# A two-layer decoder trunk: dense down projection in three split passes, and modulation sections spread over both layers

## Chip, cores and metric

The kernel runs on one core of a Trainium2 chip. The metric is the device time of one execution in microseconds (us).

## The reference

Two layers work on x, 256 tokens of 1024 channels in float32. A vector c, through silu, gives for each layer a modulation of six sections of 1024 values: `mod = silu(c) @ ada_w[l] + ada_b[l]`. Sections are numbered 6l + 0 to 6l + 5: shift, scale and gate of the mixer, then shift, scale and gate of the channel mixer.

```
for l in 0, 1:
    sh1, sc1, g1, sh2, sc2, g2 = split(mod[l], 6)
    h = rmsnorm(x) * (1 + sc1) + sh1
    x = x + g1 * hybrid_mixer(h)                 # nine 512-column projections, three gates of 1024, three branches, w_o
    h = rmsnorm(x) * (1 + sc2) + sh2
    layer 0: x = x + g2 * ((silu(h @ w1) * (h @ w3)) @ w2)       # D_FF = 2816: 22 tiles of 128
    layer 1: x = x + g2 * top-2-of-8 experts, each the same SwiGLU
out = rmsnorm(x)
```

## The kernel before, in words

Weights come from DRAM in pieces of 128x1024 float32 (512 KB). `dense_pieces` (L160) writes their order out by hand; the SP queue issues them in that order into a ring of RAW = 11 buffers (`raw`, L445 to L451), and waits before each until the piece 11 places ahead has been used up (`released`, L428). There are three kinds:

- "split" pieces. ScalarE (ACT) copies the piece to its rounded high part (L1049, called in `high_parts`), VectorE (DVE) takes the difference as the low part (L1237, in `low_parts`), both into a ring of SPL = 6 buffers (`split`); the raw buffer is free once the low part is there. TensorE (PE) then does three products for every tile: high by high, high by low, low by high (`PASSES`). A tile is one 128x128 weight block against 256 tokens, so a piece has 8 tiles and 24 matmuls.
- "ada" pieces, a 128-row part of a modulation section. DVE multiplies the piece by 128 values of silu(c) and adds to `adacc` (`product`, L1296). After eight of them PE sums over the partitions (`ada_sum`, L660) and DVE adds the bias (`modulate`, L1312). The first product of the next section waits for the sum of the last one.
- "down" pieces, the rows of w2 of layer 0, which PE reads from the raw buffer as plain float32, without a split (`next_direct`, L605; `down`, L826). The trace counts each such matmul as two instructions.

Each layer runs `norm`, then nine head groups (f, q, ab, ac, ah, i, v, u, g; four pieces each) with nine small score levels between them, then for each of three branches eight gate pieces and four branch pieces, then eight pieces of w_o. In layer 0 section 2 lies beside the head (four pieces after f, four after u), 3 and 4 beside the gates of branches c and b. Fifteen 512 KB blocks of zeros are written to DRAM in layer 1 on the same SP queue, one behind every second split piece from the first branch piece on (L452 to L455).

Layer 0 then has `dense_ffn` (L802): 11 pairs of tiles, four split pieces a pair (two of w1, two of w3), each pair followed by FFN_TAKE ada pieces: 4, 4, then 3 eight times, then 0, for the sections 5, 6, 7 and 11. A section is summed at the end of the pair after the one in which its products end. DVE first makes the low parts of the next pair, then the two products of each tile (L1605, L1607) when PE has finished the pair, then the ada products. The down projection follows: 22 pieces, with three sections (8, 9, 10) of ada pieces between them and three sums. The last four pieces are done bank by bank so that the residual add and the squares of the next norm can start early. Layer 1 has no sections of its own; its mixer and then the experts (528 pieces) follow.

PE works through two plans written out in order: units (four banks `psU`) and events (two pairs of banks `psA`); opening one waits until the one four units or two events earlier was emptied.

Of the kernel before, what the change touches and what calls it, by code (L numbers as in the profile page):

```python
# [109 lines left out]
def event_plan():  # L110

    plan = []
    for l in range(DEPTH):
# [5 lines left out]
        if l == 0:  # L119
            plan += [(("ada", s), "D") for s in (2, 3, 4)]  # L120
# [14 lines left out]
def unit_signals():  # L135
# [24 lines left out]
def dense_pieces():  # L160
# [18 lines left out]
    for l in range(DEPTH):  # L179
        for g in HEAD_GROUPS:  # L180
# [16 lines left out]
        if l == 0:  # L197
# [7 lines left out]
            for f in range(NF):  # L205
                out += [(("down", f), "ffn_w2", 0, f * P, 0, PIECE)] + ada[:DOWN_TAKE[f]]
# [13 lines left out]
DIRECT_POS = [pos for pos, p in enumerate(PIECES) if p[0][0] == "down"]  # L220
# [8 lines left out]
def program(nc, x, c, ada_w, ada_b, norm_mix_w, norm_ffn_w, w_in, conv_w, lb_logits, hgrn_norm_w,  # L229
# [3 lines left out]
    with ExitStack() as ctx:  # L233
# [25 lines left out]
        sig = sb("sig", [P, 4, 512])  # L259
        work = sb("work", [P, 10, 1024])  # L260
# [39 lines left out]
        hidden0 = work[:, 0:6, :].rearrange("p a b -> p (a b)")[:, 0:NF * T].rearrange("p (f t) -> p f t", t=T)  # L300
# [27 lines left out]
        s_down = sem("down_piece_used")  # L328
# [91 lines left out]
        def _(sp):  # L420
# [7 lines left out]
            def released(pos):  # L428
# [8 lines left out]
                elif use[0] == "mod":  # L437
                    sp.wait_ge(s_mpc, use[1] + 1)
                elif use[1] < NF - 1:
                    sp.wait_ge(s_down, use[1] + 1)  # L440
                else:
                    sp.wait_ge(s_ev, EVENT_AT["down1"] + 1)
# [63 lines left out]
        def _(pool):  # L506
# [38 lines left out]
            pool.memset(stored[:, :], 0.0).then_inc(s_ye, 1)  # L545

# [27 lines left out]
        def _(pe):  # L574
            units, events, pieces, direct = [0], [0], [0], [0]
# [28 lines left out]

            def next_direct():  # L605

                pos = DIRECT_POS[direct[0]]
                direct[0] += 1
                pe.wait_ge(s_raw[pos % RAW], 16 * (pos // RAW + 1))
                return raw[:, pos % RAW, :]  # L610
# [40 lines left out]
            def stat_pair(bank, count, j):  # L651
# [5 lines left out]
                if j == 3:  # L657
                    last.then_inc(s_ev, 1)

# [78 lines left out]
            def mixer(l):  # L738
# [25 lines left out]
                for n, b in enumerate(BRANCHES):  # L764
# [13 lines left out]
                    if l == 0 and n < 2:  # L778
                        ada_sum(2 + n)
# [4 lines left out]
                if l == 0:  # L784
                    ada_sum(4)
# [16 lines left out]
            def dense_ffn():  # L802
# [23 lines left out]
                def down(f, w, ms):  # L826
                    for m in ms:
                        last = mm(four[m // 2][:, (m % 2) * T:(m % 2 + 1) * T], w[:, m * P:(m + 1) * P],
                                  hidden0[:, f, :], f == 0 and m % 2 == 0, f == NF - 1)
                    return last  # L830

                for f in range(BANKWISE):
                    w = next_direct()
                    if f % 2 == 0:
                        pe.wait_ge(s_uD, emptied(UNITS, UNIT_AT[("ffn", f + 1)], "D"))
                    down(f, w, range(KD)).then_inc(s_down, 1)
                    if f in (6, 12, 17):
                        ada_sum(DOWN_ADA[f // 6 - 1 if f < 17 else 2])
                pe.wait_ge(s_uD, emptied(UNITS, UNIT_AT[("ffn", NF - 1)], "D"))
                ws = [next_direct() for _ in range(BANKWISE, NF)]  # L840
                for j in range(4):
                    if j == 3:
                        stat, _ = open_event((1, "norm1"))
                        for jj in range(2):
                            stat_pair(stat, 3, jj)
                    for f, w in zip(range(BANKWISE, NF), ws):
                        last = down(f, w, (2 * j, 2 * j + 1))
                        if j == 3 and f < NF - 1:
                            last.then_inc(s_down, 1)
                    last.then_inc(s_dn if j % 2 == 0 else s_ev, 1)  # L850
# [93 lines left out]
            assert (units[0], events[0], pieces[0], direct[0]) == (len(UNITS), len(EVENTS), NSPLIT, len(DIRECT_POS))  # L944
# [65 lines left out]
        def _(act):  # L1010
# [20 lines left out]
            def unit(key):  # L1031
# [4 lines left out]
                elif key[0] == "ffn":  # L1036
                    upto = min(used + 4, SIGNAL["ffn", NF - 1][2])
# [26 lines left out]
            def norm(l, second):  # L1064

                used = SIGNAL[l, "wo", 3][2] if second else SIGNAL["ffn", NF - 1][2] if l else 0
                std(early[:, 2 * l + second:2 * l + second + 1], eps[:, :], 1)
                if l and not second:
                    high_parts(used + SPL)
# [12 lines left out]
                high_parts(used + (SPL if l or second else 4))  # L1082
# [137 lines left out]
        def _(dve):  # L1220
# [20 lines left out]
            def unit(key):  # L1241
                kind, count, used = SIGNAL[key]
                upto = used + AHEAD - 1
                if key[0] in ("ffn", "mod"):
                    upto = min(upto, SIGNAL["ffn", NF - 1][2])
# [121 lines left out]
            def prepare(l, j):  # L1367
# [8 lines left out]
                settle()  # L1376
                if j == 1:
# [45 lines left out]
            def mixer(l):  # L1423
# [454 lines left out]
```

## Time and profile before

| | us |
|---|---|
| median of 3 runs | 1616.83 (1615.46 to 1622.0) |
| the profiled execution's own time | 1616.18 |
| its span in the trace | 1614.6 |
| PE busy in the span | 1553.5 (96%) |
| DVE busy | 1268.7 (79%) |
| ACT busy | 928.8 (58%) |

The profile's page gives for each engine the busy time and its share of the span, a view of 40 equal slices with one digit each, the chain of waits that ended last, and groups of instructions by line. Where a helper issues all instructions (L596 for matmuls, L1049 for ACT's copies), the tile's name tells the groups apart. Layer 0's mixer lies at about 42 to 309 us, the pairs of the dense channel mixer at 314 to 463, the down projection at 463 to 553, layer 1's mixer at 558 to 817, and the experts behind it.

### The profile page before, as it was taken

The numbers are of one execution on the slowest core, as the hardware profiler recorded it, in microseconds if no ns is written. First come the engines' busy times: TensorE is split into PE (matmuls) and PEld (weight loads), VectorE is DVE, ScalarE is ACT, GpSimd is POOL, SyncE is SP. The second block draws the span as 40 slices with busy tenths as digits, with TensorE's granted clock in tenths as the row PEclk, the third lists the DMA queues.
The fourth block names the chain that finished last, engine by engine and source line by source line (L and its number), as shares of the span: only waits on it lengthen the run. The fifth ranks groups of instructions, "written<-read, shape, count | busy, mean of one in ns | idle before, by whom it ended". The sixth has DMA issues, their size and how long they took to land.

```text
span 1614.6 us, 26010 instructions
## 1 busy us (share of the span) xinstructions
PE 1553.5 (96%) x9478; PEld 1335.6 (83%) x9478; DVE 1268.7 (79%) x1464; ACT 928.8 (58%) x1060; POOL 37.6 (2%) x45
## 2 busy tenths in 40 slices
PE   6999999899899899999979999999999999999997
PEld 5998999899898799999977777777777777777775
DVE  7786878667664559666649989989898998989897
ACT  3534544523310343544448878787777878777784
POOL 0000000000000000000003000000000000000200
PEclk7999999999999999999979999999999999999999
DMA  8943879368789734686619999999999999999993
GB/s 330 311 131 105 274 261 294 111 209 274 259 302 320 265 116 134 202 280 227 204 53 333 395 384 391 388 379 367 388 367 383 377 375 379 364 388 371 384 390 155
DMA packets 258574, 468.97 MB, mean 290 GB/s; under 512 B 15732, under 2 KB 129580, under 8 KB 258500
## 3 DMA queue, kind: packets, MB, share of 16 engines
q1 hardware_dynamic: 252608, 455.66, 79.9%
q0 software_dynamic: 3248, 11.11, 1.9%
q10 hardware_dynamic: 2644, 1.18, 0.3%
q8 instruction: 50, 0.82, 0.2%
q14 instruction: 24, 0.20, 0.0%
HBM read 453.90 MB, written 14.00 MB: 290 GB/s over the span
## 4 chain that ended last, share of the span: by engine, by line
PE 71%; DVE 6%; DMA 2%; issue 1%; ACT 1%; DVEq 0%; SPq 0%
PE psU L596 48%; PE psA L596 22%; DMA raw<-in_ffn_w_dram 2%; DVE adacc L1310 2%; PE psA L966 1%; DVE split L1237 1%; PE psU L904 0%; DVE merged L1339 0%; DVE sig L1605 0%; PE psU L926 0%; ACT split L1049 0%; DVE rstd L1333 0%; DVE split L1648 0%; DVE sc L1404 0%; DVE work L1477 0%
## 5 line engine op out<-in xcount | busy, mean ns | idle before, releaser
L1049 ACT ACTIVATE split<-raw 128x1024 fp32r<-128x1024 f32 x732 | 765.1, 1059 | 431.0 <-PE psU L596 192.6
L1648 DVE TENSOR_TENSOR split<-raw,split 128x1024 fp32r<-128x1024 f32 x528 | 615.4, 1220 | 21.1 <-ACT split L1049 19.2
L596 PE MATMUL psU<-hS,split 128*128 128x256 f32 x3936 | 493.3, 288 | 23.2 <-DVE hS L1357 13.7
L596 PEld LDWEIGHTS psU<-hS,split 128*128 128x128 f32 x3936 | 485.9, 196 | 26.6 <-issue 26.0
L596 PE MATMUL psU<-split,xE 128*104 128x512 f32 (+1 forms) x2304 | 496.6, 375 | 2.3 <-DVE xE L1775 2.3
L596 PEld LDWEIGHTS psU<-split,xE 128*104 128x104 f32 x2304 | 365.9, 168 | 119.6 <-issue 2.4
L1237 DVE TENSOR_TENSOR split<-raw,split 128x1024 fp32r<-128x1024 f32 x204 | 242.0, 1219 | 66.5 <-ACT split L1049 66.2
L596 PE MATMUL psA<-split,hidE 128*104 128x512 f32 x1056 | 249.2, 395 | 0.0
L596 PEld LDWEIGHTS psA<-split,hidE 128*104 128x104 f32 x1056 | 175.4, 168 | 63.9
L1310 DVE SCALAR_TENSOR_TENSOR adacc<-raw,cact,adacc 128x1024 f32<-128x1024 f32 x70 | 89.8, 1283 | 10.1 <-DMA raw<-in_ada_w_dram 4.9
L596 PE MATMUL psA<-work,raw 128*128 128x256 f32 x352 | 78.8, 386 | 0.5 <-DVE mod L1318 0.5
L596 PEld LDWEIGHTS psA<-work,raw 128*128 128x128 f32 x352 | 67.7, 193 | 10.0 <-DVE mod L1318 0.5
L596 PE MATMUL psU<-yS,split 128*128 128x256 f32 x576 | 70.1, 283 | 0.0
L596 PEld LDWEIGHTS psU<-yS,split 128*128 128x128 f32 x576 | 69.6, 192 | 0.0
L1806 DVE TENSOR_TENSOR hidE<-psA,hidE 128x416 fp32r<-128x416 f32 (+1 forms) x48 | 26.6, 554 | 37.7 <-ACT hidE L1049 37.7
L596 PE MATMUL psU<-split,hS 128*128 128x512 f32 x192 | 45.8, 394 | 2.2 <-DVE split L1237 2.2
L596 PEld LDWEIGHTS psU<-split,hS 128*128 128x128 f32 x192 | 35.5, 188 | 10.2 <-issue 3.0
L1136 ACT ACTIVATE sig<-psU 128x512 f32<-128x512 f32 x24 | 14.3, 595 | 50.6 <-PE psU L596 46.0
L1049 ACT ACTIVATE hidE<-psA 128x416 fp32r<-128x416 f32 (+1 forms) x48 | 23.4, 488 | 31.0 <-PE psA L966 31.0
L1186 ACT ACTIVATE sig<-psU 104x512 f32<-104x512 f32 (+1 forms) x48 | 27.0, 562 | 14.8 <-PE psU L596 14.8
L1799 DVE TENSOR_TENSOR sig<-sig,psU 104x512 f32<-104x512 f32 (+1 forms) x48 | 30.5, 635 | 3.6 <-PE psU L596 3.6
L596 PE MATMUL psA<-work 128*128 128x128 f32 x272 | 33.2, 275 | 0.0
(217 smaller groups left out, 728.3 us busy)
## 6 DMA issues: line engine op xcount, KB each, us to landing
raw<-in_moe_w_dram SPq DMA_DIRECT2D x528, 512.0 KB, 7.2
raw<-in_w_in_dram SPq DMA_DIRECT2D x120, 512.0 KB, 5.9
raw<-in_ada_w_dram SPq DMA_DIRECT2D x96, 512.0 KB, 7.4
raw<-in_ffn_w_dram SPq DMA_DIRECT2D x66, 512.0 KB, 6.0
raw<-in_w_o_dram SPq DMA_DIRECT2D x16, 512.0 KB, 6.3
token_rows<-sc SPq DMA_DIRECT2D x10, 512.0 KB, 6.9
raw<-in_w_br_a_dram SPq DMA_DIRECT2D x8, 512.0 KB, 6.8
raw<-in_w_br_c_dram SPq DMA_DIRECT2D x8, 512.0 KB, 8.5
```

The costliest lines, as they stand in the source:

```text
L596: return pe.matmul(o, a, b, start=start, stop=stop, skip_group_check=True)
L966: last = pe.transpose(T_BANKS[g % 2][:, m * CAP:(m + 1) * CAP], sig[0:CAP, 2 + g % 2, m * P:(m + 1) * P], ident[0:CAP, 0:CAP])
L1049: return act.activation(o, i, ACT.Copy)
L1136: act.activation(sig[:, j, :], bank[:, :], ACT.Sigmoid).then_inc(s_uA, 1)
L1186: act.activation(sig[0:CAP, g % 2, 0:width], psU[2 * (g % 2)][0:CAP, 0:width], ACT.Silu).then_inc(s_silu, 1)
L1237: TTN(split[:, n % SPL, 1, :], raw[:, SPLIT_POS[n] % RAW, :], split[:, n % SPL, 0, :].bitcast(F32), ALU.subtract).then_inc(s_lo, 1)
L1310: STT(adacc[:, :], raw[:, pos % RAW, :], cact[:, k:k + 1], adacc[:, :], ALU.mult, ALU.add).then_inc(s_afree, 1)
L1648: TTN(split[:, slot, 1, :], raw[:, (RAW0 + n) % RAW, :], split[:, slot, 0, :].bitcast(F32), ALU.subtract).then_inc(s_lo, 1)
L1799: TTN(sig[0:CAP, 2 + g % 2, 0:width], s, three, ALU.mult).then_inc(s_hrow, 1)
L1806: TTN(h_lo, T_BANKS[g % 2][:, 0:len(tiles) * CAP], h_hi.bitcast(F32), ALU.subtract).then_inc(s_hlo, 1)
```

## The change

Pieces of w2 become split pieces. The hidden tiles get a high part (`hid_hi`, ACT copies it) and a low part (`hid_lo`, DVE subtracts), and the down projection does three passes. ACT computes Silu itself in place of Sigmoid, so DVE has one multiply for a tile and one subtraction. The hidden tiles lie in memory that `work` and `yS` use at other times; POOL clears part of `work` before layer 1 (`s_cleared`). The last three pieces, not four, go bank by bank. Sections 8, 9 and 10 move to layer 1, at the places where 2, 3 and 4 lie in layer 0; section 11 moves beside the down projection, one ada piece behind every second piece; 5, 6 and 7 stay beside the pairs, 3, 3 and 2 pieces a pair, so that each ends with a pair. The load of the final norm's weights moves from the down projection to behind section 10.

```diff
-FFN_ADA = [5, 6, 7, 11]
-DOWN_ADA = [8, 9, 10]
-BANKWISE = NF - 4
-DOWN_TAKE = [2, 2, 1, 1, 1, 1] * 3 + [0] * (NF - 18)
+FFN_ADA = [5, 6, 7]
+DOWN_ADA = [11]
+LAST_ROWS = 3
+BANKWISE = NF - LAST_ROWS
+MOD_AT = 18
+DOWN_TAKE = [int(f % 2 == 0 and f < 2 * KD) for f in range(NF)]
-FFN_TAKE = [4, 4] + [3] * 8 + [0]
+FFN_TAKE = [3, 3, 2] * 3 + [0, 0]
...
-        if l == 0:
-            plan += [(("ada", s), "D") for s in (2, 3, 4)]
+        plan += [(("ada", 6 * l + s), "D") for s in (2, 3, 4)]
...
+            used += MOD_AT if kind == "mod" else 0
             signal[key] = ("direct", direct, used)
+            used += NF - MOD_AT if kind == "mod" else 0
...
-            if l == 0 and g == "f":
+            if g == "f":
                 two = section()
                 out += two[:4]
-            if l == 0 and g == "u":
+            if g == "u":
                 out += two[4:]
...
-            ada = section() if l == 0 and b != BRANCHES[0] else []
+            ada = section() if b != BRANCHES[0] else []
...
-                out += [(("down", f), "ffn_w2", 0, f * P, 0, PIECE)] + ada[:DOWN_TAKE[f]]
+                out += [("split", "ffn_w2", 0, f * P, 0, PIECE)] + ada[:DOWN_TAKE[f]]
...
+        with ExitStack() as ffn:
+            hid_hi = ffn.enter_context(nc.sbuf_tensor("hid_hi", [P, NF + 2, T], F32R))
+            hid_16 = ffn.enter_context(nc.sbuf_tensor("hid_16", [P, 16, T], F32R))
         work = sb("work", [P, 10, 1024])
...
-        hidden0 = work[:, 0:6, :].rearrange("p a b -> p (a b)")[:, 0:NF * T].rearrange("p (f t) -> p f t", t=T)
+        hid_lo = [hid_16[:, f, :] for f in range(16)] \
+            + [yS[:, f // HB, f % HB, :] for f in range(NF - 16)]
...
-            pool.wait_ge(s_unit, SIGNAL["mod", 10][1])
-            pool.dma_start(fwbc, final_norm_w.rearrange("(a d) -> a d", a=1).to_broadcast([P, D])).then_inc(s_fw, 16)
-
+            pool.wait_ge(s_ev, EVENT_AT["down1"] + 1)
+            pool.memset(work[:, 4:6, :], 0.0).then_inc(s_cleared, 1)
...
+            pool.wait_ge(s_ev, EVENT_AT[("ada", 10)] + 1)
+            pool.dma_start(fwbc, final_norm_w.rearrange("(a d) -> a d", a=1).to_broadcast([P, D])).then_inc(s_fw, 16)
...
-                    if l == 0 and n < 2:
-                        ada_sum(2 + n)
+                    if n < 2:
+                        ada_sum(6 * l + 2 + n)
...
-                if l == 0:
-                    ada_sum(4)
+                ada_sum(6 * l + 4)
...
-                        last = mm(four[m // 2][:, (m % 2) * T:(m % 2 + 1) * T], w[:, m * P:(m + 1) * P],
-                                  hidden0[:, f, :], f == 0 and m % 2 == 0, f == NF - 1)
+                        for wp, hp in PASSES:
+                            last = mm(four[m // 2][:, (m % 2) * T:(m % 2 + 1) * T], w[wp][:, m * P:(m + 1) * P],
+                                      hid_lo[f] if hp else hid_hi[:, f, :], f == 0 and m % 2 == 0 and (wp, hp) == (0, 0),
+                                      f == NF - 1 and (wp, hp) == PASSES[-1])
                     return last
 
                 for f in range(BANKWISE):
-                    w = next_direct()
-                    if f % 2 == 0:
-                        pe.wait_ge(s_uD, emptied(UNITS, UNIT_AT[("ffn", f + 1)], "D"))
-                    down(f, w, range(KD)).then_inc(s_down, 1)
-                    if f in (6, 12, 17):
-                        ada_sum(DOWN_ADA[f // 6 - 1 if f < 17 else 2])
-                pe.wait_ge(s_uD, emptied(UNITS, UNIT_AT[("ffn", NF - 1)], "D"))
-                ws = [next_direct() for _ in range(BANKWISE, NF)]
+                    pe.wait_ge(s_flo, f + 1)
+                    w = next_split()
+                    down(f, w, range(KD)).then_inc(s_used, 1)
+                    if f == MOD_AT - 1:
+                        ada_sum(DOWN_ADA[0])
+                pe.wait_ge(s_flo, NF)
+                ws = [next_split() for _ in range(BANKWISE, NF)]
...
+            def ffn_high(f):
+
+                act.wait_ge(s_uD, emptied(UNITS, UNIT_AT[("ffn", f)], "D"))
+                copy(hid_hi[:, f, :], sig[:, f % 4, T:2 * T]).then_inc(s_fhi, 1)
+
             for f in range(NF):
                 bank = unit(("ffn", f))
-                act.activation(sig[:, f % 4, 0:T], bank[:, 0:T], ACT.Sigmoid).then_inc(s_sig, 1)
+                act.activation(sig[:, f % 4, 0:T], bank[:, 0:T], ACT.Silu).then_inc(s_sig, 1)
+                if f:
+                    ffn_high(f - 1)
+            ffn_high(NF - 1)
+            high_parts(FFN_END + NF)
...
-                if l == 0:
-                    for k in range(4):
-                        product(2, k)
+                for k in range(4):
+                    product(6 * l + 2, k)
...
+            def ffn_low(f):
+
+                dve.wait_ge(s_fhi, f + 1)
+                TTN(hid_lo[f], sig[:, f % 4, T:2 * T], hid_hi[:, f, :].bitcast(F32), ALU.subtract).then_inc(s_flo, 1)
+
...
-                link(TTN(sig[:, f % 4, 0:T], sig[:, f % 4, 0:T], bank[:, 0:T], ALU.mult))
-                settle()
-                TTN(hidden0[:, f, :], sig[:, f % 4, 0:T], bank[:, T:2 * T], ALU.mult).then_inc(s_uD, 1)
+                TTN(sig[:, f % 4, T:2 * T], sig[:, f % 4, 0:T], bank[:, T:2 * T], ALU.mult).then_inc(s_uD, 1)
+                if f:
+                    ffn_low(f - 1)
...
+            ffn_low(NF - 1)
             modulate(FFN_ADA[-1])
-            for s in DOWN_ADA:
-                for k in range(KD):
-                    product(s, k)
-                modulate(s)
-
-            dve.wait_ge(s_eD, emptied(EVENTS, EVENT_AT[("ada", 11)], "D"))
-            low_parts(SIGNAL["ffn", NF - 1][2] + SPL)
+            done = 0
+            for f in range(NF):
+                low_parts(FFN_END + f + 1)
+                for _ in range(DOWN_TAKE[f]):
+                    product(DOWN_ADA[0], done)
+                    done += 1
+            modulate(DOWN_ADA[0])
+
+            dve.wait_ge(s_eD, emptied(EVENTS, EVENT_AT[("ada", 5)], "D"))
+            low_parts(FFN_END + NF + SPL - LAST_ROWS)
```

## Rows read from the trace of the kernel before

**Rows 1.** Windows by stage: mixer of layer 0, pairs, down projection.

```profile
core 0: us, PE busy (x) PEld busy (x) DVE busy (x) ACT busy (x) POOL busy (x), PEclk, DMA share, GB/s
42.10:308.70 266.60, 263.46 (x2076) 257.00 (x2076) 205.56 (x250) 119.26 (x141) 1.38 (x1) 0.99 0.69 223
313.60:463.20 149.60, 140.52 (x1104) 139.33 (x1104) 104.45 (x125) 48.92 (x63) 0.00 (x0) 0.94 0.69 232
463.20:553.40 90.20, 88.95 (x433) 78.12 (x432) 41.44 (x47) 11.10 (x14) 0.76 (x1) 0.98 0.85 300
```

**Rows 2.** Waits of PE, 313 to 466 us: total, times, longest.

```profile
PE psU L596 <- DVE split L1237: 8.2, 5, 3.8
```

**Rows 3.** Waits of DVE in the same stretch.

```profile
DVE mod L1318 <- PE psA L596: 6.2, 2, 3.8
```

**Rows 4.** Timeline of PE, pairs: start, length, instruction, count [idle before <- releaser].

```profile
313.70 36.60 PE L596 MATMUL psU<-hS,split 128*128 128x256 f32 x288 [5.01 <-DVE hS L1357]
...
437.61 25.70 PE L596 MATMUL psU<-hS,split 128*128 128x256 f32 x192 [3.76 <-DVE split L1237]
463.25 1.95 PE L596 MATMUL psA<-ones,adacc 128*128 128x1 f32 x16
```

**Rows 5.** Chain of waits, 400 to 421 us: start, length, step.

```profile
401.98 1.29 DVE adacc L1310
...
406.06 5.21 DMA raw<-in_ffn_w_dram
411.29 1.07 ACT split L1049
...
415.10 1.29 DVE adacc L1310
```

**Rows 6.** Timeline at the end of the last pair, all engines.

```profile
463.35 0.66 ACT L1151 ACTIVATE sig<-psU 128x256 f32<-128x256 f32 x2 [6.42 <-PE psU L596]
463.83 0.42 DVE L1605 TENSOR_TENSOR sig<-sig,psU 128x256 f32<-128x256 f32 x1 [0.64 <-ACT sig L1151]
```

**Rows 7.** Timeline of PE, down projection.

```profile
465.67 26.10 PE L596 MATMUL psA<-work,raw 128*128 128x256 f32 x112 [0.48 <-DVE mod L1318]
491.61 1.84 PE L596 MATMUL psU<-ones,adacc 128*128 128x1 f32 x16
493.31 20.97 PE L596 MATMUL psA<-work,raw 128*128 128x256 f32 x96
514.11 1.84 PE L596 MATMUL psU<-ones,adacc 128*128 128x1 f32 x16
```

**Rows 8.** Timeline of PE, layer 1, gates and branch c.

```profile
720.32 23.20 PE L596 MATMUL psU<-hS,split 128*128 128x256 f32 x192
743.36 11.68 PE L596 MATMUL psU<-yS,split 128*128 128x256 f32 x96
```

**Rows 9.** The page, costliest groups: busy, mean ns of one.

```profile
L1049 ACT ACTIVATE split<-raw 128x1024 fp32r<-128x1024 f32 x732 | 765.1, 1059 | 431.0 <-PE psU L596 192.6
L1237 DVE TENSOR_TENSOR split<-raw,split 128x1024 fp32r<-128x1024 f32 x204 | 242.0, 1219 | 66.5 <-ACT split L1049 66.2
```

**Rows 10.** Timeline of PE: first and last matmuls of mixer 0, then of mixer 1.

```profile
42.19 25.47 PE L596 MATMUL psU<-hS,split 128*128 128x256 f32 x192 [3.62 <-DVE hS L1357]
67.50 1.03 PE L859 MATMUL psU<-ident,work 128*128 128x128 f32 x8
...
307.56 1.13 PE L596 MATMUL psA<-sig,ones 128*128 128x256 f32 x4 [0.77 <-ACT sig L1078]
...
558.52 30.96 PE L596 MATMUL psU<-hS,split 128*128 128x256 f32 x240 [5.11 <-DVE hS L1357]
...
816.27 1.13 PE L596 MATMUL psA<-sig,ones 128*128 128x256 f32 x4 [0.77 <-ACT sig L1078]
```

**Rows 11.** Windows: gates b of layer 0; zero blocks of layer 1 (PE, PEclk, DMA share, GB/s).

```profile
248.00:281.00 33.00, 33.00 (x279) 33.00 (x277) 27.48 (x29) 15.11 (x18) 0.00 (x0) 1.00 1.05 341
...
733.00:738.00 5.00, 5.00 (x44) 1.00 0.95 291
```

More of the change, by code:

```diff
@@ L219 @@
 ZERO_AT = {SPLIT_POS[NSPLIT - 4 * (3 * len(BRANCHES) + 2) + 8 + 2 * n]: b for n, b in enumerate(ZERO_BLOCKS)}
-DIRECT_POS = [pos for pos, p in enumerate(PIECES) if p[0][0] == "down"]
+FFN_END = SIGNAL["ffn", NF - 1][2]
 assert len(SPLIT_POS) == NSPLIT and len(ADA_POS) == NADA * KD - len(DIRECT1 + DIRECT0)
@@ L326, in program @@
         s_out = sem("out_stored")
-        s_down = sem("down_piece_used")
+        s_fhi = sem("ffn_tile_high")
+        s_flo = sem("ffn_tile_low")
+        s_cleared = sem("level_operands_cleared")
         s_dn = sem("down_first_bank_of_pair_ready")
@@ L436, in released @@
                     sp.wait_ge(s_ev, EVENT_AT[("ada", 0)] + 1)
-                elif use[0] == "mod":
+                else:
                     sp.wait_ge(s_mpc, use[1] + 1)
[L439 to L442, printed above, removed]
             sp.wait_ge(s_small, 16 * len(stacks))
@@ L574, in _ @@
         def _(pe):
-            units, events, pieces, direct = [0], [0], [0], [0]
+            units, events, pieces = [0], [0], [0]
             def open_unit(key):
@@ L603, in next_split @@
                 return split[:, n % SPL, 0, :], split[:, n % SPL, 1, :]
[L605 to L610, printed above, removed]
             PASSES = ((0, 0), (0, 1), (1, 0))
@@ L658, in stat_pair @@
                     last.then_inc(s_ev, 1)
+                return last
             def ada_sum(s):
@@ L843, in dense_ffn @@
                         stat, _ = open_event((1, "norm1"))
-                        for jj in range(2):
-                            stat_pair(stat, 3, jj)
+                        stat_pair(stat, 3, 0)
                     for f, w in zip(range(BANKWISE, NF), ws):
[L847 to L850, printed above, removed]
+                        if j == 3:
+                            down(f, w, (6,))
+                            last = down(f, w, (7,))
+                            last.then_inc(s_used if f < NF - 1 else s_ev, 1)
+                        else:
+                            last = down(f, w, (2 * j, 2 * j + 1))
+                    if j < 3:
+                        last.then_inc(s_dn if j % 2 == 0 else s_ev, 1)
+                stat_pair(stat, 3, 1).then_inc(s_used, 1)
                 for jj in range(2, 4):
@@ L943, in _ @@
             gather(open_event("gather0")).then_inc(s_ev, 1)
-            assert (units[0], events[0], pieces[0], direct[0]) == (len(UNITS), len(EVENTS), NSPLIT, len(DIRECT_POS))
+            assert (units[0], events[0], pieces[0]) == (len(UNITS), len(EVENTS), NSPLIT)
             pe.wait_ge(s_uA, emptied(UNITS, len(UNITS), "A"))
@@ L1036, in unit @@
                 elif key[0] == "ffn":
-                    upto = min(used + 4, SIGNAL["ffn", NF - 1][2])
+                    upto = used + 4
                 if used:
@@ L1064, in norm @@
             def norm(l, second):
-                used = SIGNAL[l, "wo", 3][2] if second else SIGNAL["ffn", NF - 1][2] if l else 0
+                used = SIGNAL[l, "wo", 3][2] if second else FFN_END + NF if l else 0
                 std(early[:, 2 * l + second:2 * l + second + 1], eps[:, :], 1)
                 if l and not second:
-                    high_parts(used + SPL)
+                    high_parts(used + SPL - LAST_ROWS)
                 for j in range(4):
@@ L1081, in norm @@
                 std(rstd[:, :], bank[:, 0:T], D).then_inc(s_eA, 1)
-                high_parts(used + (SPL if l or second else 4))
+                high_parts(used + (SPL if second else 4))
                 if not (l or second):
@@ L1243, in unit @@
                 upto = used + AHEAD - 1
-                if key[0] in ("ffn", "mod"):
-                    upto = min(upto, SIGNAL["ffn", NF - 1][2])
                 if used:
@@ L1376, in prepare @@
                 settle()
+                if l and j == 1:
+                    dve.wait_ge(s_cleared, 1)
                 if j == 1:
@@ L1514, in ada_part @@
                 def ada_part(n, ks):
-                    gates = SIGNAL[(0, "gate" + BRANCHES[n], 0)][2] - 2
-                    if l == 0:
-                        for k in ks:
-                            if n:
-                                low_parts(gates + k + 1)
-                            product(2 + n, k)
+                    gates = SIGNAL[(l, "gate" + BRANCHES[n], 0)][2] - 2
+                    for k in ks:
+                        if n:
+                            low_parts(gates + k + 1)
+                        product(6 * l + 2 + n, k)
                 ada_part(0, range(4, KD))
@@ L1576, in mixer @@
                                 merged_low(3)
-                    if l == 0 and n < 2:
-                        modulate(2 + n)
-                if l:
-                    unit_done(("mod", 8))
-                else:
-                    modulate(4)
-                    dve.wait_ge(s_eD, emptied(EVENTS, EVENT_AT[("ada", 2)], "D"))
+                    if n < 2:
+                        modulate(6 * l + 2 + n)
+                modulate(6 * l + 4)
+                dve.wait_ge(s_eD, emptied(EVENTS, EVENT_AT[("ada", 6 * l + 2)], "D"))
                 for j in range(4):
```

## The prediction

> **What bounds the kernel now.** I read the page first: PE is busy for 96% of the span, so only PE's own work, its waits and its clock can move the end. I then cut the span into stages with the windows view [rows 1]; the reader is to see that the mixer of layer 0 has PE busy for nearly all of its 266.6 us at a clock of 0.99, while the pairs of the dense channel mixer have 9.1 us without PE work and a clock of 0.94. PE's waits in that stretch name the low parts of the weights, 8.2 us in five waits [rows 2]. DVE's own waits say why: twice it stood before `modulate` until PE had summed a section, 6.2 us [rows 3]. That is a section that ended in the middle of a pair: its sum runs only after the next pair, and until then DVE makes no low parts and frees no ada buffer. The chain of waits shows the second limit, a loop of 13.1 us a pair (401.98 to 415.10: three products, 5.21 us from the last release to the landing of a piece, the high part, the low part, the tiles) against the 11.5 us that PE needs [rows 5]. In the down projection PE hardly waits at all; there the work itself is the time.
>
> **Pace of PE.** At full clock 192 split matmuls of 128x256 take 743.36 - 720.32 = 23.04 us, 0.120 us each [rows 8]. The plain float32 ones of the down projection take 514.11 - 493.31 = 20.80 us for 96, 0.217 each, and there are two in the trace for each matmul written [rows 7]. A section's sum costs 493.31 - 491.61 = 1.70 us [rows 7].
>
> **The pairs (313.7 to 463.25, 149.5 us).** Work that stays: 1056 matmuls x 0.120 = 126.7; three sums (5, 6, 7), 5.1; the start, where 288 matmuls took 36.60 in place of 34.56, 2.0 [rows 4]. Together 133.8, so 15.7 us are waits and the slow clock behind them. The price of one such clock dip: behind the 3.76 us wait the last 192 matmuls took 463.25 - 437.61 = 25.64 us, 2.6 more than at full clock [rows 4, 8]. With 3, 3 and 2 ada pieces each section ends with a pair and the next one starts a pair later, when its sum follows directly: the 6.2 us on DVE go. In the loop, the buffer for the fourth split piece two pairs on is freed by the third product in a pair (3, 3), by the second in (3, 2), and by the second of two in (2, 3); so two of three pairs have a loop shorter by 1.29 + 0.1, 11.7 us, and three pairs take 13.1 + 2 x 11.7 = 36.5 us against 3 x 11.5 + 1.7 = 36.2 of PE. That is even, and the first pairs have some slack, so I keep 4.5 us of residue (3.0 of waits, 1.5 of clock; bounds 0 and 12). The new ACT copies and DVE subtractions lie beside this: DVE still has two operations of 0.42 us a tile, and ACT is busy for 48.9 of 149.6 us and gets 22 copies of about half of 1.06 us or less [rows 1, 6, 9]; were the cover gone, their 22 x 0.5 = 11 us would show. After: 138.3. Gain 11.2.
>
> **The turn to the down projection.** PE opens its banks after `modulate(7)`, which now stands behind the last low part. Before, 465.67 - 463.25 = 2.42 us passed, with the sum of 11 inside [rows 4, 7]. Now the chain from 463.35 is: two Silus and the high copy between them, about 1.2 us; the last high copy and the latency around it, 0.6; the last subtraction 0.42; `modulate` 0.2; handing over, 0.6. That makes 3.2 us (bounds 2.4, and 4.5 if each copy takes as long as 0.66 us). PE comes out of it at a lower clock as behind a 3.76 us wait: 2.6 us.
>
> **The down projection (463.2 to 553.4, 90.2 us).** Removed: 352 x 0.217 = 76.4 at the steady pace (with the slow first group 465.67 to 491.61 it was 78.0), 5.1 for three sums, the 2.4 above. What is left, 4.7, is norm statistics and the last residual add, which stay. Added: 22 pieces x 24 matmuls x 0.120 = 63.4, one sum 1.7. After: 3.2 + 2.6 + 63.4 + 1.7 + 4.7 = 75.6, gain 14.6 (bounds 12 and 16). ACT's 22 x 1.06 = 23 us and DVE's 22 x 1.22 + 8 x 1.3 = 37 us [rows 5, 9] lie beside 63 us of PE; the transfers fall from 46 to 30 pieces in that stage, and a raw buffer is now freed when it is split, not when PE has used it. If the split were not hidden, a piece would cost 1.06 + 1.22 = 2.3 us, still under PE's 2.88. Three pieces held for the bank-wise end leave three of six split buffers for layer 1 where before all six were ready; layer 0 starts in that very way.
>
> **Layer 1.** Added: 24 products on DVE, 24 ada pieces in the queue, three sums on PE, a move of the ring's release by ada pieces. Layer 0 runs the same code with its sections already, so it is the nearest row: from its first matmul to the last statistic 308.69 - 42.19 = 266.50 us, in layer 1 817.40 - 558.52 = 258.88 [rows 10]. The difference is 7.6; of it 1.0 is the turning of the gating weights, which stays in layer 0. So +6.6, of which 5.1 are sums and the rest the start with fewer pieces ready. Layer 1 has besides fifteen blocks of zeros in the same queue, which layer 0 has not. I add 1.4 for them (bounds 0 and 29, below). POOL's clearing and the moved load of the final norm have tens of us before their users wait; SP and POOL are not passed by anything on PE's path. Sum: +8.0.
>
> **Sum.** 1616.18 - 11.2 - 14.6 + 8.0 = 1598.4 against the profiled execution's own time, which stands 0.65 under the median of the runs; I say 1599.
>
> **Zero blocks and a rule.** Beside the gates of branches c and b layer 1 will ask for 8 gate pieces, 8 ada pieces and 4 zero blocks each, 20 x 0.524 = 10.5 MB in 23.0 us. In layer 0, without zero blocks, the transfer engines are already full over such a stretch, share 1.05 at 341 GB/s [rows 11]; at that rate each takes 30.8 us, 7.7 too many. The lookahead covers it: eleven raw buffers, half of them split pieces, and up to five pieces split ahead, some ten pieces or 29 us, and behind each gate group four branch pieces with two zero blocks need only 9.2 of 11.5 us. The Trainium skill, page "DMA: Bandwidth & Descriptors", section "Specifications", speaks against the change here: it gives a core a limit of about 358 GB/s from HBM. By that rule a group would take an estimated 29.3 us, 6.3 too many, which by itself, without lookahead, makes 12.6 for both in place of the 15.4 that the row gives; the row's 341 is a little below the rule and I go by the row.
>
> **Rivals.** (A) The loop in the pairs stays as it is: 13.1 us a pair, because landings grow with the new order. For it: the landing is 5.2 us in one loop and set by what else is in flight. Against: fewer pieces, and no sums in mid-pair. Then the pairs gain about 3 in place of 11.2: 1607. (B) The zero blocks eat half of the lookahead: half of 15.4 in place of 1.4 and one clock dip, +9: 1608. For it: share 1.05 in layer 0; against: the ten pieces ahead. (C) Slower: with reads and writes mixed, the rate at the gates of layer 1 drops to the 291 GB/s of a five-us window among the zero blocks, with a share of 0.95 [rows 11]. A group then takes 36.0 us, 13 too many, 26 for both, and with the lookahead used up two dips of 2.6: +31 in place of 1.4, 1628. It decides from a stall of 19 us on (no faster) or 27 (slower by 0.5%). Against it: that window follows a pause in the releases, so its rate is not a limit. (D) The change does not do what it says: weights are loaded 528 times in place of 352, and if a load of about 0.19 us were not hidden, the down projection would take 528 x 0.19 = 100 us, 37 more: 1636. The same loads stand in the gates, at 0.120 a matmul [rows 8], so hardly.
>
> **Chances.** Forecast 0.72 (own range 1591 to 1606), A 0.12, B 0.09, C 0.05, D 0.02. A measurement of this kernel can tell about 0.5%, 8.1 us, from no change, so faster means under 1608.7. The forecast is faster throughout, A and B about two times in three: 0.72 + 0.14 = 0.86; same 0.09, slower 0.05. The range 1590 to 1609 takes in A and B.
>
> **What would show it.** Pairs: about 138 us with a clock near 0.98, and no wait of DVE on a sum; over 145 means A. Between the last pair's matmul and the first of the down projection 3 us. Down projection: 528 matmuls at 0.12, stage about 76. Layer 1 from its first matmul to the last statistic 267; over 275, with PE waiting for low parts beside `ada` or w_in landings at the gates, means B or C. Experts and layer 0 unchanged. I am wrong in the main step if the three passes run slower than 0.125 each, or if PE waits again for DVE between pieces of w2.

## The result and the profile after

The changed kernel takes 1591.04 us (median of 4 runs, 1590.47 to 1591.6) against 1616.14 us for the kernel before beside it: ratio 0.9844, 95% interval 0.9831 to 0.9857. The forecast was 1599; the way and the mechanism were right, the gain is 25 us where 17 were forecast.

The page of the changed kernel, its first part: busy time, share of the span, instructions.

```profile
span 1588.4 us, 26461 instructions
PE 1533.6 (97%) x9654; PEld 1325.9 (83%) x9654; DVE 1291.2 (81%) x1486; ACT 959.7 (60%) x1104; POOL 39.5 (2%) x46
```

PE's timeline over the pairs, to be laid beside [rows 4] (start, length, count, idle before):

```profile
314.16 48.01 PE L602 MATMUL psU<-hS,split 128*128 128x256 f32 x384 [5.01 <-DVE hS L1369]
362.00 1.84 PE L602 MATMUL psA<-ones,adacc 128*128 128x1 f32 x16
363.71 34.79 PE L602 MATMUL psU<-hS,split 128*128 128x256 f32 x288
...
436.37 11.75 PE L602 MATMUL psU<-hS,split 128*128 128x256 f32 x96
450.82 0.55 PE L602 MATMUL psA<-hid_hi,split 128*128 128x256 f32 x1 [2.69 <-DVE mod L1330]
...
454.80 0.40 PE L602 MATMUL psA<-hid_hi,split 128*128 128x256 f32 x2
```

From the first matmul of the pairs to their last there is no idle time left; the only wait behind that is the 2.69 us before the down projection. PE's waits there, the same stage in windows, and the chain of waits from 330 to 448 us, which is PE's own work alone, say it again (compare [rows 2] and [rows 1]):

```profile
PE psU L602 <- DVE hS L1369: 5.0, 1, 5.0
PE psA L602 <- DVE mod L1330: 2.7, 1, 2.7
```

```profile
314.00:448.10 134.10, 133.94 (x1104) 133.63 (x1104) 97.02 (x119) 60.13 (x86) 0.00 (x0) 0.99 0.75 255
```

```profile
by line: PE psU L602 95.8%; PE psA L602 4.3%
```

The end of the down projection, and the first and last matmuls of layer 1's mixer (compare [rows 7] and [rows 10]):

```profile
514.67 1.02 PE L602 MATMUL psA<-sig,ones 128*128 128x256 f32 x4
...
517.67 2.92 PE L602 MATMUL psA<-sig,ones 128*128 128x256 f32 x12
525.70 10.60 PE L602 MATMUL psU<-hS,split 128*128 128x256 f32 x72 [5.11 <-DVE hS L1369]
...
790.27 1.13 PE L602 MATMUL psA<-sig,ones 128*128 128x256 f32 x4 [0.76 <-ACT sig L1082]
```

Read from these rows and those of before, the span's 26.2 us (1614.6 to 1588.4) come apart like this:

| stage | before | forecast | after | moved |
|---|---|---|---|---|
| up to the first matmul of the pairs | 313.70 | 313.70 | 314.16 | +0.5 |
| pairs | 149.55 | 138.3 | 133.96 | -15.6 |
| turn and down projection to the last statistic | 90.2 | 75.6 | 72.5 | -17.7 |
| from there to layer 1's first matmul | 5.1 | 5.1 | 5.1 | 0 |
| layer 1, first matmul to last statistic | 258.88 | 266.9 | 265.70 | +6.8 |
| rest (routing, experts, end) | 797.2 | 797.2 | 797.0 | -0.2 |

### The profile page after: what moved, and what is told of

Read it like the earlier page. It is cut to its first block, busy times and chain, and to the rows that moved or that the text cites. A ratio compares the mean times of both kernels' runs of the same rounds, so it can differ in the third digit from the quotient of the medians.

```text
span 1588.4 us, 26461 instructions
## 1 busy us (share of the span) xinstructions
PE 1533.6 (97%) x9654; PEld 1325.9 (83%) x9654; DVE 1291.2 (81%) x1486; ACT 959.7 (60%) x1104; POOL 39.5 (2%) x46
## 4 chain that ended last, share of the span: by engine, by line
PE 74%; DVE 5%; issue 1%; ACT 0%; DVEq 0%
PE psU L602 51%; PE psA L602 22%; PE psA L970 1%; DVE split L1251 1%; DVE adacc L1322 0%; DVE merged L1351 0%; PE psU L908 0%; PE psU L930 0%; DVE rstd L1345 0%; DVE split L1666 0%; DVE sc L1418 0%; DVE work L1490 0%; DVE hS L1369 0%; DVE work L1870 0%; DVE work L1402 0%
## 5 line engine op out<-in xcount | busy, mean ns | idle before, releaser
L1053 ACT ACTIVATE split<-raw 128x1024 fp32r<-128x1024 f32 x754 | 788.2, 1059 | 378.3 <-PE psU L602 178.3
L1666 DVE TENSOR_TENSOR split<-raw,split 128x1024 fp32r<-128x1024 f32 x528 | 615.4, 1220 | 21.4 <-ACT split L1053 19.4
L602 PE MATMUL psU<-hS,split 128*128 128x256 f32 x3936 | 488.0, 286 | 16.3 <-DVE hS L1369 13.7
L602 PEld LDWEIGHTS psU<-hS,split 128*128 128x128 f32 x3936 | 480.6, 194 | 19.2 <-issue 18.2
L1251 DVE TENSOR_TENSOR split<-raw,split 128x1024 fp32r<-128x1024 f32 x226 | 268.7, 1219 | 66.1 <-ACT split L1053 65.6
L602 PE MATMUL psA<-hid_hi,split 128*128 128x256 f32 x352 | 64.9, 286 | 2.7 <-DVE mod L1330 2.7
L602 PEld LDWEIGHTS psA<-hid_hi,split 128*128 128x128 f32 x352 | 55.5, 193 | 2.9 <-DVE mod L1330 2.9
L602 PE MATMUL psA<-hid,split 128*128 128x256 f32 x128 | 36.6, 286 | 0.0
```

The lines of the kernel that those rows point to most:

```text
L602: return pe.matmul(o, a, b, start=start, stop=stop, skip_group_check=True)
L1053: return act.activation(o, i, ACT.Copy)
L1251: TTN(split[:, n % SPL, 1, :], raw[:, SPLIT_POS[n] % RAW, :], split[:, n % SPL, 0, :].bitcast(F32), ALU.subtract).then_inc(s_lo, 1)
L1666: TTN(split[:, slot, 1, :], raw[:, (RAW0 + n) % RAW, :], split[:, slot, 0, :].bitcast(F32), ALU.subtract).then_inc(s_lo, 1)
```

## The experiments

For a short comparison of all kernels, their traces are cut at three marks: D is the time from the first matmul of the pairs to ACT's square root behind the down projection (`rstd`), L from there to the same mark at the end of layer 1's mixer. The ratio is to the kernel before beside each. D and L come from one profile of each kernel. They hold some chance: the first 384 matmuls of the pairs, the same instructions with no wait among them, took 48.01 us in the change, 48.79 in e4 and e7, and 49.19 in e5, so a difference of up to 1.2 us in D need not be an edit's doing.

| kernel | median | ratio (95% interval) | D | L |
|---|---|---|---|---|
| before | | 1 | 239.8 | 264.0 |
| the change | 1591.04 | 0.9844 (0.9831 to 0.9857) | 206.5 | 270.8 |
| e1 three passes alone | 1621.34 | 1.0027 (1.0016 to 1.0038) | 246.1 | 264.0 |
| e1b the same, DVE's order capped | 1622.91 | 1.0042 (1.0028 to 1.0055) | 246.4 | 263.6 |
| e1c the same, ada pieces spread | 1612.61 | 0.998 (0.9969 to 0.999) | 235.3 | 264.2 |
| e2 sections alone | 1604.82 | 0.9927 (0.9908 to 0.9946) | 220.5 | 270.8 |
| e3 3 pieces a pair, ends in mid-pair | 1600.9 | 0.9898 (0.9875 to 0.9922) | 217.7 | 270.8 |
| e6 4 pieces a pair, ends on borders | 1607.74 | 0.995 (0.9932 to 0.9968) | 222.7 | 270.8 |
| e4 modulate(7) early | 1588.05 | 0.9825 (0.9807 to 0.9844) | 204.2 | 270.9 |
| e7 modulate(7) behind pair 9 | 1587.22 | 0.9817 (0.9802 to 0.9831) | 202.3 | 271.6 |
| e5 zero blocks twice | 1599.7 | 0.9895 (0.9878 to 0.9912) | 207.7 | 279.0 |
| e8 second statistic early | 1592.2 | one run | 208.0 | 270.8 |

### e1: the three passes alone

The changed kernel with the sections put back:

```
-FFN_ADA = [5, 6, 7]
-DOWN_ADA = [11]
-MOD_AT = 18
-DOWN_TAKE = [int(f % 2 == 0 and f < 2 * KD) for f in range(NF)]
-FFN_TAKE = [3, 3, 2] * 3 + [0, 0]
+FFN_ADA = [5, 6, 7, 11]
+DOWN_ADA = [8, 9, 10]
+MOD_AT = {8: 7, 9: 13, 10: 18}
+DOWN_TAKE = [2, 2, 1, 1, 1, 1] * 3 + [0] * (NF - 18)
+FFN_TAKE = [4, 4] + [3] * 8 + [0]
...
-                for k in range(4):
-                    product(6 * l + 2, k)
+                if l == 0:
+                    for k in range(4):
+                        product(2, k)
```

> The down projection in three passes, with the modulation sections placed as before (5, 6, 7, 11 beside the pairs; 8, 9, 10 beside the down projection; none in layer 1). Theory 1 (the two parts of the change add up, and each saves PE time by itself): the pairs stay at 149.5 us, the down projection falls from 90.2 to about 78 (63.4 of matmuls, 5.1 for three sums, turn, statistics), so 12 us less than before, 1604. Theory 2 (the sections have to go before three passes can pay): DVE has 22 low parts and 24 products there, 58 us, and their order and landings hold PE up; PE waits for low parts of w2 for 5 us or more and the kernel stays at 1609 or above.

Measured: 1621.34, slower than the kernel before. Theory 1 fell. The time is in the range of theory 2, which put it down to DVE's order and the landings; the next two kernels take these apart. PE's waits from 313 to 560 us:

```profile
PE psA L605 <- DVE mod L1335: 10.9, 1, 10.9
PE psU L605 <- DVE split L1256: 9.1, 6, 3.8
PE psA L605 <- DVE split L1256: 7.5, 2, 6.3
```

The waits in the pairs (second row) are those of before; the 10.9 us before the down projection and the 7.5 us in it are new. DVE's timeline there (start, length, count):

```profile
502.47 0.16 DVE L1335 TENSOR_TENSOR mod<-psU,vecs 128x8 f32<-128x8 f32 x1
502.54 0.75 DVE L1324 TENSOR_SCALAR adacc<-raw,cact 128x1024 f32<-128x1024 f32 x1
503.39 8.23 DVE L1327 SCALAR_TENSOR_TENSOR adacc<-raw,cact,adacc 128x1024 f32<-128x1024 f32 x6
511.54 1.22 DVE L1256 TENSOR_TENSOR split<-raw,split 128x1024 fp32r<-128x1024 f32 x1
```

Reading a section's bank (`unit`) first makes low parts up to four pieces ahead, and then the products of those pieces come in a row: nine microseconds without a low part, longer than PE's ready pieces last.

### e1b: the same with DVE's order capped

```
             def unit(key):
                 kind, count, used = SIGNAL[key]
                 upto = used + AHEAD - 1
+                if key[0] in ("ffn", "mod"):
+                    upto = min(upto, FFN_END)
```

> As e1, but DVE makes no low part of w2 ahead of the tiles of the last pair and none ahead of its products when it turns to a section's sum (the cap that the kernel before had in unit() stays). Theory 1 (e1 lost its gain to DVE's order: 10.9 us before the down projection and 7.5 us beside it while six products ran in a row): the wait before the down projection falls to 4 us or less, the waits between pieces of w2 below 3 us, the kernel comes to about 1606 to 1610. Theory 2 (24 products and 46 transfers beside the down projection cannot keep up with 2.88 us a piece in any order): the waits move but stay above 12 us together and the kernel stays above 1614.

Measured: 1622.91, no better: the numbers are those of theory 2 (waits above 12 us, time above 1614). The products no longer come six in a row, but the wait before the down projection is still 9.3 us (row: total, times, longest), and so theory 1's account of it, DVE's order, was wrong:

```profile
PE psA L605 <- DVE split L1256: 16.4, 3, 9.3
```

SP's queue and ACT in e1b around the end of the last pair, which PE leaves at 464.3 us:

```profile
462.30 0.33 SPq L458 DMA_DIRECT2D raw<-in_ffn_w_dram  x1
462.68 0.43 SPq L458 DMA_DIRECT2D raw<-in_ada_w_dram  x1
463.15 0.43 SPq L458 DMA_DIRECT2D raw<-in_ffn_w_dram  x1
...
467.78 1.06 ACT L1058 ACTIVATE split<-raw 128x1024 fp32r<-128x1024 f32 x1 [6.35 <-DMA raw<-in_ffn_w_dram]
470.63 1.06 ACT L1058 ACTIVATE split<-raw 128x1024 fp32r<-128x1024 f32 x1 [1.79 <-DMA raw<-in_ffn_w_dram]
471.59 0.36 ACT L1166 ACTIVATE sig<-psU 128x256 f32<-128x256 f32 x1
```

The third and fourth pieces of w2 are issued at 462.30 and 463.15, when the last pair is nearly over. With the sections of before, five ada pieces stand between the first four pieces of w2. So in a ring of eleven the third one needs the buffer of the last ada piece before the last pair, whose product ends at 462.27, and the fourth stands behind it in the queue. ACT makes high parts four pieces ahead before it turns to a tile, so the Silu of the last pair (471.59), and with it the whole turn, waits until the fourth piece has landed at about 470.6. The plain float32 reading of before split no piece of w2, so nothing stood in front of the tiles.

### e1c: the same with the ada pieces spread

```
-MOD_AT = {8: 7, 9: 13, 10: 18}
-DOWN_TAKE = [2, 2, 1, 1, 1, 1] * 3 + [0] * (NF - 18)
+MOD_AT = {8: 9, 9: 15, 10: 19}
+DOWN_TAKE = [0, 0] + [2, 1, 1, 1, 1, 1, 1] + [2, 1, 1, 2, 1, 1] + [2, 2, 2, 1, 1] + [0, 0]
```

> As e1b, but the 24 ada pieces beside the down projection are spread over pieces 2 to 19 of w2, none behind the first two, and each sum comes when DVE is just through with its section. Theory 1 (e1 and e1b lost to ada pieces between the first four pieces of w2, which set the wait before the down projection, and to bunched products): that wait falls from 9 us to about 3, the waits between pieces to 5 us or less, the kernel to 1608 to 1612. Theory 2 (46 transfers, 24.1 MB, and 58 us of DVE do not fit into 63 us of matmuls in this ring, however spread): PE waits stay above 12 us together, 1615 or more.

Measured: 1612.61, 0.998 of before. Theory 1 is nearly met, and theory 2 fell: from 463 to 545 us PE waits for low parts of w2 for 8.2 us in all, 5.4 us of it at the turn, where theory 1 said 3:

```profile
PE psA L605 <- DVE split L1256: 8.2, 6, 5.4
```

The order was worth 10 us, but no order that was tried brings the 12 us that the matmuls alone save.

### e2: the sections alone

On the kernel before, with the plan of the change for the sections (constants as in the diff, `ada_sum(6 * l + ...)`, `product(6 * l + ...)`, `modulate(6 * l + ...)`), w2 in plain float32 and four pieces bank by bank. Only the start of layer 1 has another number, since ada pieces now stand behind its first four split pieces:

```
-            low_parts(SIGNAL["ffn", NF - 1][2] + SPL)
+            low_parts(SIGNAL["ffn", NF - 1][2] + 3)
```

> The sections placed as in the change, the down projection left in plain float32 with four pieces bank by bank. Theory 1 (waits and slow clock in the pairs come from the placement of the sections): the pairs fall from 149.5 to about 134, the down projection loses two sums (3.4 us), layer 1 gains 6.8; together 12 us less than before, 1604. Theory 2 (the shorter vector chain of a tile, with Silu on ACT, is what freed the pairs): the pairs stay above 142, the kernel at 1610 or above.

Measured: 1604.82, as theory 1 has it. PE's timeline of the pairs is that of the change, with the two multiplies of a tile of before:

```profile
313.92 47.98 PE L594 MATMUL psU<-hS,split 128*128 128x256 f32 x384 [5.01 <-DVE hS L1354]
361.74 1.84 PE L594 MATMUL psA<-ones,adacc 128*128 128x1 f32 x16
363.44 34.79 PE L594 MATMUL psU<-hS,split 128*128 128x256 f32 x288
```

So the placement freed the pairs, not Silu. With e1 this shows that the two parts do not add up: sections alone -19.3 us in D, three passes alone +6.3 (-4.5 in e1c's order), both together -33.3. On top of the new placement the three passes bring 14.0.

### e3 and e6: where a section ends, and how many pieces a pair takes

```
-FFN_TAKE = [3, 3, 2] * 3 + [0, 0]
+FFN_TAKE = [3] * 8 + [0, 0, 0]          # e3
+FFN_TAKE = [4, 4] * 3 + [0] * 5         # e6
```

> The changed kernel with 3 ada pieces behind each of the first eight pairs in place of 3, 3, 2 behind nine: as many pieces in all, but sections 5 and 6 end in the middle of a pair. Theory 1 (DVE stands before a sum that comes only after the next pair): DVE waits on PE before modulate in two places, PE waits for low parts behind them for some 4 to 6 us with a slow clock after it, pairs at 140 to 145, the kernel 6 to 10 us above the change. Theory 2 (only the number of ada pieces per pair matters, by the loop): one piece less in the loop is all that 3, 3, 2 had; no wait on a sum, 0 to 2 us above the change.

> The changed kernel with 4 ada pieces behind each of the first six pairs and none behind the other five: sections end on pair borders, but the loop from product to tile is one product longer. Theory 1 (only the sums in mid-pair made PE wait; the loop of 14.4 us is drawn against slack and ends after six pairs): no wait of DVE on a sum, 0 to 3 us above the change. Theory 2 (the loop sets the pace, as the prediction's residue of 4.5 us had it): 14.4 against 11.5 us a pair over six pairs, PE waits for low parts 6 us or more, the kernel 8 us or more above the change.

e3 measured 1600.9, 10 us above the change: theory 1. DVE's and PE's waits in e3's pairs:

```profile
DVE mod L1330 <- PE psA L602: 11.0, 2, 6.0
```

```profile
PE psU L602 <- DVE split L1251: 6.4, 3, 3.5
```

Two sections end in mid-pair, and there are two waits of DVE on a sum; D grows by 11.2 us, of which 6.4 are PE's waits. The other 4.8 are for the most part the low clock behind them: the 192 matmuls behind the waits of 2.15 and 3.54 us took 24.75 and 25.84 us, where [rows 8] has 23.20.

e6 measured 1607.74, 17 us above the change. Theory 1 fell and theory 2 holds: no wait of DVE on a sum, but the loop costs more than the mid-pair ends. PE's waits and a piece of the chain in e6 (start, length, step):

```profile
PE psU L602 <- DVE split L1251: 10.5, 4, 3.1
```

```profile
333.38 1.30 DVE adacc L1322
334.69 0.37 SPq L455
335.11 7.34 DMA raw<-in_ffn_w_dram
342.48 1.06 ACT split L1053
...
350.20 1.30 DVE adacc L1322
```

The loop takes 350.20 - 333.38 = 16.8 us, not the 14.4 of both theories: four products free four buffers one after the other, and the piece that counts lands after 7.3 us, where it was 5.2 in [rows 5]. In the kernel before, too, the pieces behind the four products of its first two pairs land after 7.27 and 6.54 us. That the piece then stands behind others in the queue is the likely reason; no run isolates it. Both limits that the prediction named are real; the change clears both at once.

### e4 and e7: the turn to the down projection

```
                 TTN(sig[:, f % 4, T:2 * T], sig[:, f % 4, 0:T], bank[:, T:2 * T], ALU.mult).then_inc(s_uD, 1)
+                if f == NF - 2:                 # e4
+                    modulate(FFN_ADA[-1])
                 if f:
                     ffn_low(f - 1)
+                if f == NF - 3:                 # e7, in place of the one above
+                    modulate(FFN_ADA[-1])
...
             ffn_low(NF - 1)
-            modulate(FFN_ADA[-1])
```

> The changed kernel with DVE's modulate(7) moved from behind the last low part of the hidden tiles to the first tile of the last pair, where its sum has long been there. Theory 1 (PE's 2.7 us before the down projection are the chain up to modulate, which only frees a bank, and the slow clock behind it costs about 1 us more): PE starts the down projection within 0.7 us of the last pair, the kernel is 3 to 4 us below the change. Theory 2 (the first pieces of w2 or the low part of the hidden tiles set the start): 0 to 1 us.

> The changed kernel with modulate(7) right behind the tiles of the last but one pair, so that nothing of the last pair stands before PE's start on the down projection. Theory 1 (only the bank's release held PE; the first hidden tiles and pieces of w2 are long ready): PE goes on within 0.2 us, 4 us below the change and 1 us below e4. Theory 2 (the first pieces of w2 or DVE's wait for the sum take its place): as e4 or slower.

Both as theory 1 has them, e4 with 1.1 us of waiting left instead of 0.7. PE's wait in e4:

```profile
PE psA L602 <- DVE mod L1330: 1.1, 1, 1.1
```

The clock behind the wait, first in the change, then in e4 (us, PE busy, clock, transfer share, GB/s):

```profile
448.20:453.20 5.00, 2.38 (x11) 0.76 0.14 13
```

```profile
448.20:453.20 5.00, 4.47 (x38) 1.00 0.17 35
```

In e7 PE goes from the last pair, whose last matmul ends at 448.2, into the down projection with no wait at all:

```profile
448.07 0.28 PE L602 MATMUL psA<-hid_hi,split 128*128 128x256 f32 x1
```

D is 4.2 us under the change's, although e7's first 384 matmuls took 0.8 us more. From the end of the pairs to the square root it is 5.0 us (448.12 to 520.63 in the change, 448.22 to 515.77 in e7). Of these 2.7 are the wait. The clock is 1.6: the change's first 20 matmuls behind the wait take from 450.82 to 454.80, 3.98 us in place of 2.4. The rest is a slightly quicker pace at full clock that e4 does not have, so it is not the edit's. At 0.9817 it is the fastest kernel of the study; its interval overlaps e4's.

### e5: the room in layer 1's queue

```
                     sp.dma_start({"x": xrows, "y": yrows}[table][row:row + P, :], scf[:, 0:D]).then_inc(s_fill, 16)
+                    again = ZERO_BLOCKS.index((table, row)) * P
+                    sp.dma_start(morerows[again:again + P, :], scf[:, 0:D]).then_inc(s_fill, 16)
```

> The changed kernel with each block of zeros in layer 1 written twice, the second time to rows of its own that nobody reads: 15 more transfers of 512 KB in the stretch of the gates. Theory 1 (the transfers of layer 1 are covered by the lookahead, with room left): 0 to 3 us above the change, PE waits for weights in layer 1 stay below 6 us. Theory 2 (the rate near 341 GB/s is already used up beside the gates, rival B of the prediction nearly happened): 15 x 0.524 MB / 341 GB/s = 23 us more transfer time, of which 10 us or more show.

Measured: 1599.7, 9 us above the change, between the two: 8.2 in L. PE's waits in layer 1, and the windows of the stretch (us, busy times, clock, transfer share, GB/s):

```profile
PE psU L605 <- DVE split L1254: 8.2, 3, 5.9
```

```profile
660.00:755.00 95.00, 88.24 (x719) 87.92 (x720) 69.27 (x72) 36.95 (x42) 0.00 (x0) 0.96 1.01 380
```

One wait of 5.9 us is new, late in the stretch; the other 2.3 us are two waits that the change has too. Behind the new wait the next 96 matmuls take 13.51 us in place of 11.75, so the low clock makes most of the rest of the 8.2. Of 7.9 MB more, 21 us at 380 GB/s, more than half still did not show. Not only the lookahead took it up: in the change SP issues nothing from 681.1 to 692.0 us, since it waits for a buffer, and the transfers stand nearly still (share 0.17, 40 GB/s):

```profile
685.00:695.00 10.00, 10.00 (x87) 10.00 (x87) 6.59 (x9) 2.12 (x2) 0.00 (x0) 1.00 0.17 40
```

As an estimate, 21 less 8 us at 1.4 us a transfer, the change has room for some nine more transfers.

### e8: the order of the statistics

```
                         stat_pair(stat, 3, 0)
+                        stat_pair(stat, 3, 1)
...
-                stat_pair(stat, 3, 1).then_inc(s_used, 1)
-                for jj in range(2, 4):
-                    stat_pair(stat, 3, jj)
+                stat_pair(stat, 3, 2).then_inc(s_used, 1)
+                stat_pair(stat, 3, 3)
```

> The changed kernel with the second statistic of the norm again ahead of the last bank's matmuls, as in the kernel before. Theory 1 (three statistics behind the last matmul fill the time in which DVE and ACT make the last squares, which was 0.77 us of waiting): a wait of PE of 0.8 us on ACT's squares comes back and the stage from the last pair to the last statistic takes 0.8 to 1 us more than in the change. Theory 2 (the shorter stage comes from elsewhere): no such wait, no difference.

In e8's PE waits the one of before is back, and PE's timeline shows what it costs:

```profile
PE psA L602 <- ACT sig L1082: 0.8, 1, 0.8
```

```profile
515.10 1.89 PE L602 MATMUL psA<-sig,ones 128*128 128x256 f32 x8
...
518.95 1.02 PE L602 MATMUL psA<-sig,ones 128*128 128x256 f32 x4
520.75 1.13 PE L602 MATMUL psA<-sig,ones 128*128 128x256 f32 x4 [0.77 <-ACT sig L1082]
```

From the first statistic to the end of the last it is 515.10 to 521.88, 6.8 us, against 514.67 to 520.59, 5.9 us, in the change, with the same matmuls between: 0.9 us, as theory 1 has it. The whole stage from the last pair on takes only 0.4 us more, since the matmuls before it ran a little quicker. D is 208.0 against 206.5, but 1.1 of these 1.5 us lie in the first 384 matmuls of the pairs (49.13 against 48.01) and have nothing to do with the edit.

## Why the prediction was right, and where it was off

- **The bound.** Right: PE's waits and clock in the pairs and its work in the down projection are where the time went. Layer 0 and the experts moved by 0.5 and 0.2 us.
- **The pairs.** Mechanism right, size off. Of the 15.7 us named as waits and slow clock all 15.6 went; the residue of 4.5 us was not there. The step that mis-sized it is the loop, "13.1 + 2 x 11.7 = 36.5 us against 3 x 11.5 + 1.7 = 36.2". It treated a loop that is as long as PE's work as one that must stall; the chain of the change from 330 to 448 us is PE's own work alone. That the first pairs give slack and the last two have no ada pieces is the likely reason, which no run shows by itself. e6 shows that the loop is no phantom: one product more in it costs 17 us, and its landing is longer behind four products than behind three. e3 shows the other half, sums in mid-pair. That DVE's new tile chain would cost nothing was right (e2 has the old one and the same pairs).
- **The turn.** 2.70 us for 3.2. It was rightly seen as `modulate(7)` behind the low parts. The clock behind it cost 1.6 us, less than the 2.6 taken from the last pairs of before. e7, which has neither, is 5.0 us shorter in the stage.
- **The down projection.** 63.4 us of matmuls was close: from 450.82 to 520.59 it is 69.8 us, and without 1.6 of slow clock, 1.7 for the sum and 3.6 for the statistics 62.9 are left, 0.119 for each of 528. The stage holds no waits. The statistics were called unchanged at 4.7 us and take 517.67 to 520.59 and 0.67 before, 3.6: three stand behind the last matmul now and fill a wait of 0.77 us. e8 brings that wait back. Turn 0.5, clock 1.0, matmuls 0.5 and statistics 1.1 make the 3.1 us.
- **That the split would be hidden.** Right for this placement, but the reason given, 60 us of DVE and ACT beside 63 of PE, was not enough: e1 has the same instructions on ACT, and on DVE 16 products more, and is slower than before. Cover by busy time is no cover when the ring decides which piece lands first.
- **Layer 1.** +6.8, where layer 0's row gave 6.6 and 8.0 was forecast. The 1.4 us for the zero blocks was not needed. PE waits for low parts there for 2.5 us in all, as in layer 0 (2.3), so the zero blocks are covered, with the margin that e5 measured. What covers them is the lookahead, as argued, and besides it the pauses in which the queue waits for a buffer.
- **The rivals.** A and B did not happen, but each came near: e6 is A, called up by one more product, and e5 is B, called up by doubling the zero blocks; C (a rate of 291 GB/s) is excluded by windows of the change in that stretch (GB/s last):

```profile
665.00:675.00 10.00, 10.00 (x85) 9.98 (x85) 10.00 (x9) 4.60 (x6) 0.00 (x0) 1.00 1.05 397
...
705.00:715.00 10.00, 10.00 (x86) 10.00 (x85) 10.00 (x9) 5.58 (x8) 0.00 (x0) 1.00 1.06 393
```

D is excluded by the pace: weight loads stay hidden. The rule of the Trainium skill that was weighed ("DMA: Bandwidth & Descriptors", "Specifications", about 358 GB/s from HBM for a core) is not a limit here: these windows stand at 397 and 393 with reads and writes mixed, and the measurement decides. That row gets its figure by halving the bandwidth of a stack between two cores; this program runs on one. The row of 341 was too low as a limit as well.

What stays open: how much of D in e1c is the ring and how much DVE's load, since no kernel with three passes and 24 ada pieces beside them was tried with a longer ring.

## What to carry to other kernels

Do not add up the parts of a change: here one part alone was slower than before, and worth 14 us once the other had cleared the queue. In a ring of buffers with two kinds of users, count for each critical piece which piece must be used up before it can be issued; that, and not busy time, says whether a longer preparation is hidden. End an accumulated run where its sum comes right behind the work that is in flight, and look for short instructions, like the `modulate` here, that free a resource and stand behind work they do not need.

## What the runs showed of the hardware

- The transfer engines of the one core carried 397 and 393 GB/s over 10 us windows beside the gates of layer 1, and 380 on average over 95 us in e5, at a share of 1.01 to 1.06.
- The landing of the piece that a loop waits for is not a constant: 5.21 us in the kernel before behind three products, 7.27 and 6.54 behind four, and 7.34 behind four in e6.
- Behind a wait of PE of 2.7 us the granted clock fell to 0.76 over 448.2 to 453.2 us and cost 1.6 us more (the change); behind one of 1.1 us it stayed at 1.00 (e4). One of 3.76 us had cost 2.6 in the kernel before.
